# Cached memory keys: loaded in 32-float pieces and turned in 32x32 blocks by VectorE, in a streaming transformer layer on one core

## The reference, cut to what matters

```python
def cross_attend(h, mk, mv, p):
    q = (h @ p['w_xq']).reshape(B, T, X_HEADS, X_HEAD_DIM)
    s = jnp.einsum('bthd,bmhd->bhtm', q, mk).astype(jnp.float32) * X_SCALE
    pr = jax.nn.softmax(s, axis=-1)
    o = jnp.einsum('bhtm,bmhd->bthd', pr.astype(mv.dtype), mv).reshape(B, T, X_WIDTH)
    return o @ p['w_xo']
```

## Time and profile before

| | |
|---|---|
| times of three runs | 1524.87, 1525.36, 1526.36 us; median 1525.36 us |
| the profiled execution: its own time | 1524.94 us |
| its span, first to last instruction | 1523.1 us |
| TensorE busy | 1466.7 us, 96% of the span |
| VectorE busy | 552.6 us, 36% |
| ScalarE busy | 313.2 us, 21% |
| moved by DMA | 483.48 MB, mean 317 GB/s |

### The profile page before, as it was taken

The page is one execution under the profiler, slowest core; times in us unless marked ns, Lnnn a source line. Parts: engine busy times, 40 slices in busy tenths (PEclk is TensorE's granted clock), DMA queues, the critical chain, the costliest instruction groups (busy, mean ns, idle before and its releaser), DMA issues.

```text
span 1523.1 us, 21869 instructions
## 1 busy us (share of the span) xinstructions
PE 1466.7 (96%) x8246; PEld 720.5 (47%) x8247; DVE 552.6 (36%) x1240; ACT 313.2 (21%) x676; POOL 45.4 (3%) x55
## 2 busy tenths in 40 slices
PE   8999899999999998999999999999999999999996
PEld 7766577655687653333333333333333333333332
DVE  4245444110302365333343333343333433333334
ACT  1225555210001441111111111111111111111111
POOL 0000000160000000000000000000000000000000
PEclk9999999999999998999999999999999999999998
DMA  9411466942332468999999999999999999999994
GB/s 287 131 67 47 116 184 215 304 156 86 111 125 83 153 259 360 427 427 429 428 428 429 430 428 428 428 430 389 431 428 428 429 429 429 428 429 429 429 428 199
DMA packets 83037, 483.48 MB, mean 317 GB/s; under 512 B 18144, under 2 KB 46080, under 8 KB 56368
## 3 DMA queue, kind: packets, MB, share of 16 engines
q1 hardware_dynamic: 68800, 471.78, 75.7%
q0 software_dynamic: 3168, 9.11, 2.6%
q10 hardware_dynamic: 11024, 1.96, 0.8%
HBM read 475.16 MB, written 4.65 MB: 315 GB/s over the span
## 4 chain that ended last, share of the span: by engine, by line
PE 79%; DMA 16%; DVE 2%; ACT 1%; issue 1%; SPq 0%; DVEq 0%; ACTq 0%
PE bank L529 74%; DMA ring<-in_w_gu 16%; PE bank L1283 1%; PE bank L683 1%; PE bank L1203 1%; DMA ring<-in_w_in 1%; PE bank L920 0%; PE bank L806 0%; PE bank L694 0%; PE bank L1066 0%; DVE small L1666 0%; PE bank L543 0%; DVE ring L1677 0%; PE bank L961 0%; DVE xr L1987 0%
## 5 line engine op out<-in xcount | busy, mean ns | idle before, releaser
L529 PE MATMUL bank<-ring,hT 128*64 128x512 f32 (+3 forms) x3648 | 814.1, 567 | 14.8 <-DMA ring<-in_w_gu 13.9
L529 PEld LDWEIGHTS bank<-ring,hT 128*64 128x64 f32 (+1 forms) x3648 | 305.6, 145 | 438.7 <-issue 387.8
L1945 DVE SCALAR_TENSOR_TENSOR xr<-bank,probTs,xr 128x512 f32<-128x512 f32 x198 | 139.2, 745 | 231.1 <-PE bank L529 231.1
L529 PE MATMUL bank<-hT,ring 128*128 128x384 f32 x384 | 124.4, 487 | 0.0
L2334 ACT ACTIVATE probTs<-hT 128x512 f32<-128x512 f32 x33 | 20.8, 629 | 412.4 <-DVE hT L1964 412.4
L1982 DVE TENSOR_TENSOR mlaT<-bank,foxT 128x512 f32<-128x512 f32 x33 | 22.8, 692 | 224.6 <-ACT foxT L2340 224.6
L529 PEld LDWEIGHTS bank<-hT,ring 128*128 128x128 f32 x384 | 72.9, 190 | 50.2 <-issue 0.2
L529 PE MATMUL bank<-ring 128*128 128x256 f32 (+7 forms) x434 | 84.9, 396 | 3.8 <-issue 2.5
L529 PE MATMUL bank<-foxT 64*128 64x512 bf16 x600 | 82.2, 380 | 0.8 <-ACT foxT L2340 0.8
L529 PEld LDWEIGHTS bank<-ring 128*128 128x128 f32 (+3 forms) x434 | 59.0, 171 | 20.0 <-issue 11.5
L2340 ACT CAST foxT<-bank 128x512 bf16<-128x512 f32 x33 | 19.3, 585 | 215.7 <-PE bank L529 215.7
(11 more groups left out here) (330 smaller groups left out, 1270.8 us busy)
## 6 DMA issues: line engine op xcount, KB each, us to landing
ring<-in_w_gu SPq DMA_DIRECT2D x128, 2048.0 KB, 24.1
ring<-in_w_down SPq DMA_DIRECT2D x64, 2048.0 KB, 26.5
ring<-in_w_in SPq DMA_DIRECT2D x16, 1024.0 KB, 11.5
ring<-in_cache_fox_k SPq DMA_DIRECT2D x8, 1024.0 KB, 4.8
ring<-in_cache_fox_v SPq DMA_DIRECT2D x8, 1024.0 KB, 7.7
ring<-in_cache_mla_ckv SPq DMA_DIRECT2D x8, 512.0 KB, 5.6
ring<-in_w_out SPq DMA_DIRECT2D x4, 1024.0 KB, 5.1
ring<-in_cache_mem_k SPq DMA_DIRECT2D x8, 512.0 KB, 3.2
```

What stands on the lines that cost most here:

```text
L529: return pe.matmul(o, l, r, start=start, stop=stop, skip_group_check=True)
L1945: v.scalar_tensor_tensor(x, sums[i % 2][:, :], gate_e[:, i // 2, e], x, ALU.mult, ALU.add).then_inc(shares_added, 1)
```

## The change

Each batch's keys come by 16 DMAs in place of one. DMA (h, j) takes from all 256 rows the 32 floats `32j..32j+31` of head h, and puts row 32i+r into partition 32j+r, columns `256h+32i..`. Each 32x32 block of the slot's first 1024 columns is thus a block whose transpose is the block wanted in `xkT`. DVE makes all of them in one `transpose` of 128x1024 from the slot into `xkT[b % 2]`. TensorE's `mem_turn`, its two banks per batch, and the copies on DVE and ACT go. The values come by one DMA as before, in runs of 2 KB in place of 4 KB, since the order of the rows is now plain.

```diff
-            tile(("cm", b), [(lambda s: kview(s, 2, FW), d["cache_mem_k"][0, b].rearrange("(p k) h n -> p k (h n)", k=2)),
-                             (lambda s: ring[:, s, 1024:2048].rearrange("p (k n) -> p k n", k=2),
-                              d["cache_mem_v"][0, b].rearrange("(p k) h n -> p k (h n)", k=2))])
+            src = d["cache_mem_k"][0, b].rearrange("(i r) h (j c) -> h j r i c", r=32, c=32)
+            parts = []
+            for h in range(XH):
+                for j in range(4):
+                    parts.append((lambda s, h=h, j=j: ring[32 * j:32 * j + 32, s, MEM * h:MEM * h + MEM].rearrange("p (i c) -> p i c", c=32),
+                                  src[h, j, :, :, :]))
+            parts.append((lambda s: ring[:, s, 1024:2048].rearrange("p (k n) -> p k n", k=2),
+                          d["cache_mem_v"][0, b].rearrange("(k p) h n -> p k (h n)", k=2)))
+            tile(("cm", b), parts)
...
-            def mem_turn(b):
...
             def mem_scores(b):
-                for hh in range(2):
-                    pe.wait_ge(free(("cK", b, hh)), count(("cK", b, hh)))
+                pe.wait_ge(mem_turned, b + 1)
...
-            mem_turn(0)
...
-                    mem_turn(1)
...
-                if b == 1:
-                    mem_turn(2)
...
-                if 2 < b + 1 < NB:
-                    mem_turn(b + 1)
...
             def mem_out(b):
                 if b >= 2:
                     dve.wait_ge(full(("cS", b - 2)), count(("cS", b - 2)))
-                ps = take(("cK", b, 0))
-                give(v.tensor_copy(xkT[b % 2][:, 0:2, :], ps[:, :].rearrange("p (h s) -> p h s", h=2)), ("cK", b, 0))
+                key = ("cm", b)
+                dve.wait_ge(ring_loaded[slot(key)], loaded_at[place[key]])
+                v.transpose(xkT[b % 2].rearrange("p h s -> p (h s)"), ring[:, slot(key), 0:1024]).then_inc(mem_turned, 1)
```

More of the change, by code:

```diff
@@ L319, in build @@
         krope_ready = sem("krope_ready")
+        mem_turned = sem("mem_turned")
         ckv_ready = sem("ckv_ready")
@@ L1058, in _ @@
                 used_last(pe, i, ("xq", j))
-            def mem_turn(b):
-                s = arrived(pe, ("cm", b))
-                k3 = kview(s, 2, FW)
-                for hh in range(2):
[L1063 to L1068, removed]
             def mem_scores(b):
-                for hh in range(2):
-                    pe.wait_ge(free(("cK", b, hh)), count(("cK", b, hh)))
+                pe.wait_ge(mem_turned, b + 1)
                 if b == 0:
@@ L2231, in _ @@
                 copy_out(("xq", h), xqT[:, h, :], TOK)
[L2233 to L2237, removed]
             def mem_exps(b):
@@ L2271, in cross_squares @@
                 squares(2 * NT + 2 + t, xr[:, t, :], junk=mlaf[:, 0:D])
-            mem_out(0)
             act.wait_ge(bias_moved, 96)
             def between_units(i):
-                if i == 1:
-                    mem_out(1)
                 if i == 2:
@@ L2291, in _ @@
                     mem_outputs(b - 2)
-                if 1 < b + 1 < NB:
-                    mem_out(b + 1)
                 if 1 <= b <= NB:
```

## The result

The changed kernel takes 1539.28 us (median of 4 runs, 1535.80 to 1540.14) against 1525.11 us for the kernel before, run beside it (4 runs, 1524.68 to 1526.36). The ratio is 1.0087, with a 95% interval of 1.0070 to 1.0105: slower by 14.2 us, where the sum of the prediction has 5.5 + 0.7 = 6.2 us. The profiled execution took 1539.34 us, its span 1537.5 us, against 1524.94 and 1523.1 us before; so the two traces can be compared directly, and 14.4 us are to be found between them.

The account below looks back on a forecast made before the run. TensorE, then the weight stream, paces the experts; before the table, TensorE from batch to batch, then SP's issuing. 1524.94 + 5.5 (table late) + 0.7 (clock) = 1531.1 us; range 1520 to 1548, if slower 1528 to 1541.

Parts of the forecast that it names:

- The sign: Whole kernel: slower, chance 0.63; same 0.20, faster 0.17.
- The pitch: SP's issues of cached keys and values for tiles 3 to 7: 0.49 us each, bounds 0.37 and 0.74 us.
- The start: SP issues tile 3 from 508.2 us, after two turnings ahead of it give 0.87 and 0.5 us.
- Landing and transpose: Before batch 7's scores: 3.5 us from last issue to landing, 1.1 us DVE transpose, 0.2 us semaphore.
- What goes: TensorE's path: eight turnings of keys at 0.87 us, 7.0 us in all, with bank copies on DVE and ACT beside.
- Rival 4: TensorE stays the bound and all 7.0 us are saved, 1517.9 us; chance 0.03.
- The tail: From batch 7's scores to the table: 0.5 us gained from ACT work done earlier, 0.7 us lost to the clock.
- The weights: First expert weight tile issued behind tile 7's last issue, at 549.9 us instead of 539.42; no loss there.
- that SP's pitch is 0.37 us: Rival: SP's issues have the pitch of one alone, giving 1520.4 us; chance 0.14.
- that nothing changes (0.39 to 0.46 us): Rival: at this pitch the table stays within 3 us of now, around 1525 us; chance 0.20.
- pace the issue at 0.74 us: Rival: short pieces set SP's pitch, batch 7's scores at 575.2 us, 1551.4 us; chance 0.15 with what lies between.
- The rule weighed in the prediction: Skill's rule on DMA transfers: coalesce those below 64 KB; each new one has 32 KB, so the pieces' price decides.

Follow-up runs that it names:

- the runs with all and with half the fillings: The changed kernel with extra matmuls ahead of TensorE's waits for keys of batches 4 to 7: 2, 14, 12, 22 (1544.85 us) or 1, 8, 7, 11 (1538.55 us).
- the third experiment: The changed kernel with each batch's keys in one DMA in the old layout, DVE's transpose kept: 1523.17 us, ratio 0.9980.
- fourth experiment: The changed kernel with 2, 14, 12 and 22 extra matmuls ahead of the waits for keys of batches 4 to 7: 1544.85 us, ratio 1.0122.
- the second and third experiments: The second: the kernel before, TensorE's turning kept, each batch's keys in 16 DMAs of 32 pieces of 1 KB: 1534.23 us, ratio 1.0064.
- first experiment: The changed kernel with each batch's keys in 4 DMAs in place of 16, the same 4096 pieces: 1522.88 us, ratio 0.9976.
- The long-piece runs: Keys in 16 DMAs of 32 pieces of 1 KB: in the kernel before, 1534.23 us; in the changed kernel with DVE's transpose, 1535.30 us.

## Why the prediction was right in kind and short in size

The sign, the mechanism and the place were as forecast: SP issues without a pause from 510 us, DVE waits for the DMA, TensorE for DVE, the table comes late, and the expert stage keeps its length. The size was not: 14.2 us for 6.2 us forecast. The time still lies within the 1528 to 1541 us stated for slower, because of the room given to the pitch. The measured pitch alone would make it 1534.7 us; the start and the way behind the scores, for which the range left nothing, bring the rest. By the prediction's own steps:

- **The pitch, the term of the sum that was mis-sized.** The undisturbed pitch was right: 0.49 us, made of an issue of 0.45 and 0.04 between. The sum took it as the mean. With the stalls of single issues the mean is 0.5315 us, and 84 x 0.0415 = 3.5 us are missing. The earlier trace rows had four issues in a row, too few to show a stall. In the runs with all and with half the fillings, whose DMAs are the same, SP's mean was 0.529 and 0.538 us, so this isn't a chance of one execution.
- **The start.** Tile 3 was issued from 510.17 us, not 508.2. 1.46 us of that stood already ahead of everything that the change touches: the first cached keys were sent at 438.06 us against 436.60. It varies from execution to execution (436.37 to 438.06 us over the profiles here), and what makes it was not traced; that it fell out late here is chance. The other 0.5 us is the turning beside the copy of the last query tile: it was thought to give half of itself and gives nothing; only one of the two ahead of tile 3 does, as the third experiment has it.
- **Landing and transpose.** 3.66 us for 3.5, and 1.25 us for the 1.1 that I took. The Trainium skill, Vector Engine (DVE) Microarchitecture Reference, section 3.8, gives one element per cycle per lane; the estimate made from it was 1.07 us for 1024 columns. The trace has 1.25 us, somewhat above the estimate and close to the 1.23 us of a plain operation on 1024 columns. Neither was on a scale to matter.
- **What goes.** Eight turnings were booked at 7.0 us. In this kernel, with DVE's transpose in their place, they are worth 4.75 us up to batch 7's scores and 3.3 us of the whole time (third experiment). It cost the forecast little, as TensorE was not the bound in batches 4 to 7. Rival 4's 1517.9 us were out of reach with it: with SP's cost gone the third experiment has 1523.17 us.
- **The tail**, from batch 7's scores to the table. Forecast were a gain of 0.5 us and a loss of 0.7 to the clock, 0.2 us together; measured was a loss of 2.17 us up to the first expert matmul. With the granted clock at 0.56 in 560 to 565 us, so mostly at 1.2 GHz, the scores take 1.08 us instead of 0.62, the eight transposes at 561.58 us 1.91 instead of 1.04, and the second part of the router's logits is copied 569.40 - 559.88 = 9.52 us after the scores, where it was 555.81 - 548.13 = 7.68. From this copy on DVE sets the pace: it comes to the last `cross_add` (581.16 us) 11.76 us later, before (567.58 us) 11.77, after what it makes out of x, the last of it at 578.75 us. The last projection starts 11.06 us after the scores instead of 9.37 and then takes 8.83 us for 9.95, but TensorE can't use the 1.1 us: it stands 2.17 us until DVE is through, where it stood 0.91. The later copy makes 1.8 of the 2.17 us; the other 0.3 come behind 581.94 us. With the waits filled and the clock up the same stretch lost 0.4 us (fourth experiment), so the clock is what most of the 2.17 us hang on; the size is from single traces. The windows for this (columns as in the earlier trace rows), which answer to the earlier trace rows:

```profile
555.00:560.00 5.00, 0.12 (x4) 0.12 (x8) 1.39 (x3) 1.41 (x3) 0.00 (x0) 0.75 0.94 337
560.00:565.00 5.00, 5.00 (x31) 4.19 (x31) 2.55 (x7) 1.05 (x4) 0.00 (x0) 0.56 1.00 423
```

- **The weights.** They were issued at 555.39 us, forecast 549.9, and were no bound: the first expert matmul waited for the table's side, and the expert stage has the same 939 us in the change, in the kernel before and in the second and third experiments (941 in the first).

Added up: 1.97 us (start), 3.5 (pitch) and 0.2 (landing and transpose) make batch 7's scores 5.7 us later than forecast; the tail adds 2.0 and the expert stage 0.5. That is the 8.2 us between 1531.1 and 1539.3.

**The rivals.** That TensorE stays the bound, that SP's pitch is 0.37 us and that nothing changes (0.39 to 0.46 us) all fell with the pitch measured. The pieces do not pace the issue at 0.74 us; they add 0.04 us when each DMA has 256 of them. With 1024 in a DMA the issue takes 1.0 to 1.5 us when queued (first experiment), so there the pieces do count, at another size. The rule weighed in the prediction, the Trainium skill, DMA: Bandwidth & Descriptors, Rules for kernel authors, that transfers below 64 KB pay mostly overhead, agrees with this case in its direction: 32 KB transfers cost SP 0.46 to 0.49 us whether their pieces have 1 KB or 128 bytes, and 128 KB transfers with the same short pieces, though each cost 1.0 to 1.5 us, made the kernel faster than before.

## What to carry to other kernels

A DMA split into many has a price on the issuing queue, here some 0.49 us for each, stalls included, beside the 0.04 us that short pieces add; multiply the count by it and set it against the time that the consumer needs per tile. If the issuing queue comes out slower, the work saved elsewhere is worth nothing. Put a dimension inside the access pattern of one DMA rather than into a loop over DMAs: here that alone turned 0.9% slower into 0.2% faster. And before booking removed work at its full length, look at what each instance stands beside: of eight equal transposes three had other waits next to them.

## What the runs showed of the hardware

- Issues of 32 KB made in a row take about the same time in long and in short pieces: with 32 pieces of 1 KB the quiet issue is 0.42 us and the next follows 0.04 us later, with 256 pieces of 128 bytes 0.45 and 0.04. Sixteen in a row, undisturbed, are 7.40 and 7.87 us. With 1024 pieces of 128 bytes (128 KB) an issue in a row takes 1.0 to 1.5 us.
- Single issues of SP stall and take 0.8 to 1.8 us, with long pieces (1.12 us at 516.84, 1.32 at 532.73) and with short ones (0.83 at 514.97, 1.64 at 521.84, 1.82 at 534.90). In the changed kernel's trace one packet of a queue of the kind "instruction" (q8) runs in 521 to 523 us and one in 534.5 to 536.5 us, the same places. The long-piece runs have it too: one at 516.3 to 516.6 us ahead of the 1.12 us, one at 532.7 to 533.3 us in the 1.32 us. The 0.83 us at 514.97 has none beside it, and packets of the other instruction queue (q14) run where no issue stalls. Whether these packets are the cause was not tested.
- DVE's transpose of 32x32 blocks takes 1.25 us for 128x1024 in fp32, about as long as an elementwise operation on as many columns (1.23 us).
- A batch of 512 KB in 4096 pieces of 128 bytes, in four DMAs, beside 512 KB of values, took 5.9 us of SP and kept the DMA engines some 90% busy. With SP ahead of TensorE the last five still came in time for iterations of 4.92 us.
- The granted clock fell to 0.50 for 10 us also where no wait for keys came before (third experiment, 550 to 560 us).
